# Four chunk operands written in front of the taking of the bonus sum

## The reference

```python
zd = z + mu[d] * (shift_seq(z, offset) - z)            # mixed r, k, v
kk = kk * lax.rsqrt(maximum(sum(kk * kk), 1e-24))      # normed keys
k = k * (1.0 + (a - 1.0) * k_a)
seqs = [r, decay, k, v, -kk, kk * a]                   # go into the scan
bonus = sum(r * k * r_k, axis=-1) * v                  # goes past the scan
```

## Time and profile before

| | us |
|---|---|
| runs, median of 3 (lowest, highest) | 3369.15 (3364.13, 3369.31) |
| profiled execution: span from the first to the last instruction | 3357.8 |
| median of the runs less this span | 11.35 |
| TensorE (PE) busy in the span | 3114.1 (93%) |
| weight loads (PEld) busy | 2493.0 (74%) |
| VectorE (DVE) busy | 1500.2 (45%) |
| ScalarE (ACT) busy | 1162.7 (35%) |
| GpSimd (POOL) busy | 831.6 (25%) |
| mean granted clock of TensorE, share of full speed | 0.976 |

### The profile page before, as it was taken

The page is one execution under the profiler, slowest core; times in us unless marked ns, Lnnn a source line. Parts: engine busy times, 40 slices in busy tenths (PEclk is TensorE's granted clock), DMA queues, the critical chain, the costliest instruction groups (busy, mean ns, idle before and its releaser), DMA issues.

```text
span 3357.8 us, 79208 instructions
## 1 busy us (share of the span) xinstructions
PE 3114.1 (93%) x34382; PEld 2493.0 (74%) x34382; DVE 1500.2 (45%) x2358; ACT 1162.7 (35%) x2403; POOL 831.6 (25%) x518
## 2 busy tenths in 40 slices
PE   7999898999999998999999888989899989989998
PEld 5777676778777786888888666767667667768886
DVE  4455473745444653100144464756565456330033
ACT  4433333423334424211112353434333345342222
POOL 2211111111123132222223221111111243434453
PEclk9999999999999999999999989999999999999999
DMA  5424242434454441111111233413233343522222
GB/s 212 135 97 145 81 142 101 130 121 144 145 166 151 158 169 57 51 63 62 62 50 63 75 101 98 127 63 120 65 122 106 93 140 115 188 69 95 99 88 75
DMA packets 246714, 364.56 MB, mean 109 GB/s; under 512 B 154080, under 2 KB 155376, under 8 KB 245904
## 3 DMA queue, kind: packets, MB, share of 16 engines
q1 hardware_dynamic: 226976, 294.57, 27.6%
q10 hardware_dynamic: 14976, 35.66, 2.7%
q0 software_dynamic: 4464, 29.92, 2.5%
HBM read 290.88 MB, written 69.21 MB: 107 GB/s over the span
## 4 chain that ended last, share of the span: by engine, by line
PE 76%; DVE 6%; issue 5%; ACT 4%; DMA 2%; DVEq 2%; POOLq 2%; PEld 1%; SPq 1%; POOL 0%; PEldq 0%; ACTq 0%
PE banks L281 20%; PE banks L282 18%; PE banks L283 18%; PE banks L1684 2%; PE banks L1023 2%; PE banks L1695 1%; PE banks L1648 1%; PE banks L395 1%; PE banks L1687 1%; PE banks L1745 1%; POOLq L2430 1%; DVE arena L597 1%; PE banks L2057 1%; PE banks L1051 1%; DMA arena<-chunk_inputs 1%
## 5 line engine op out<-in xcount | busy, mean ns | idle before, releaser
L283 PE MATMUL banks<-hx_rounded,slot_rounded 128*128 128x512 f32 (+1 forms) x1624 | 575.1, 354 | 0.0
L906 POOL TENSOR_TENSOR slot_rounded<-slot,branch_weights_high 128x512 fp32r<-128x512 f32 x188 | 251.4, 1357 | 1286.2 <-ACT branch_weights_high L901 1284.9
L281 PE MATMUL banks<-hx_high,weight_parts 128*128 128x512 f32 (+1 forms) x1512 | 537.9, 356 | 10.9 <-DVE hx_low L545 10.4
L281 PE MATMUL banks<-hx_rounded,branch_weights_high 128*128 128x512 f32 (+1 forms) x1280 | 498.8, 390 | 48.1 <-DVE arena L1364 8.6
L282 PE MATMUL banks<-hx_low,weight_parts 128*128 128x512 f32 (+1 forms) x1512 | 538.0, 356 | 0.0
L283 PE MATMUL banks<-hx_high,weight_parts 128*128 128x512 f32 (+1 forms) x1512 | 535.9, 354 | 0.0
L282 PE MATMUL banks<-resid_rounded,branch_weights_high 128*128 128x512 f32 (+1 forms) x1280 | 452.7, 354 | 0.0
L283 PEld LDWEIGHTS banks<-hx_rounded,slot_rounded 128*128 128x128 f32 x1624 | 312.2, 192 | 44.3
L281 PEld LDWEIGHTS banks<-hx_rounded,branch_weights_high 128*128 128x128 f32 x1280 | 245.9, 192 | 128.2 <-issue 75.6
L281 PEld LDWEIGHTS banks<-hx_high,weight_parts 128*128 128x128 f32 x1512 | 286.6, 190 | 55.1 <-issue 14.3
L283 PEld LDWEIGHTS banks<-hx_high,weight_parts 128*128 128x128 f32 x1512 | 286.3, 189 | 41.1
(11 more groups left out here) (263 smaller groups left out, 5853.7 us busy)
## 6 DMA issues: line engine op xcount, KB each, us to landing
slot<-in_w_mix SPq DMA_DIRECT2D x120, 512.0 KB, 3.9
slot<-in_w_ffn_in SPq DMA_DIRECT2D x88, 512.0 KB, 3.3
arena<-chunk_inputs SPq DMA_DIRECT2D x48, 640.0 KB, 4.5
arena<-in_w_ada SPq DMA_DIRECT2D x50, 512.0 KB, 5.1
slot<-in_w_ffn_out SPq DMA_DIRECT2D x44, 512.0 KB, 3.3
slot<-in_w_ada SPq DMA_DIRECT2D x40, 512.0 KB, 4.3
chunk_inputs<-arena SPq DMA_DIRECT2D x80, 256.0 KB, 3.9
arena<-side_projections POOLq DMA_DIRECT2D x16, 1152.0 KB, 6.1
```

Source lines behind the costliest of these rows:

```text
L281: first = nc.tensor.matmul(out, w_hi, x_hi, start=start, stop=False)
L283: return first, nc.tensor.matmul(out, w_lo, x_hi, start=False, stop=stop)
L906: last = nc.gpsimd.tensor_tensor(slots_r[g % 3][:, half], slots[g % 3][:, half], weights_high(g)[:, half], ALU.subtract)
```

## The change

In both directions of every preparation, the four no longer wait for the gap of the bonus. A generator, bonus_taken(until), is called in front of each of them and at the end. It emits the taking (line 1418's instructions, unchanged) at the first call whose bound is not below the bonus's gap; the last call, with 999, emits it in any case. So the taking stands in front of the first of the four whose own gap is not below the bonus's, or behind all four. g now goes on from line 1409's gap. A drain is put in front of the last sum (line 1434). The drain between lines 1427 and 1431, the semaphores and their counts, and the order on the other engines' programs stay.

```diff
                 for d in range(2):
                     k = 8 * d
+                    bonus_left = list(enumerate([s for s in sum_order(l, st, d == 0) if s in outs]))
+
+                    def bonus_taken(until):
+                        while bonus_left and at(("bonus", d)) <= until:
+                            i, s = bonus_left.pop(0)
+                            yield max(g, at(("bonus", d)))
+                            (c0, c1), (t0, t1) = SEGS[s], TSEG[s]
+                            dst = bonus(hq)[:, c0:c1] if d == 0 else TMP[6][:, c0:c1]
+                            dve.wait_ge(pre_prod.sem, pre_prod.ready(l, hq, k + 7 + i))
+                            nc.vector.tensor_tensor(dst, pair(6)[s], TMP[2][:, t0:t1], ALU.mult).then_inc(pre_dve.sem, both_done)
+
...
                     nc.vector.tensor_tensor(TMP[1], TMP[1], E2, ALU.mult).then_inc(made.sem, 1)
 
-                    assert g < at(("bonus", d)), (st, hp, d, g, at(("bonus", d)))
-                    g = at(("bonus", d))
-                    yield g
-                    for i, s in enumerate([s for s in sum_order(l, st, d == 0) if s in outs]):
-                        (c0, c1), (t0, t1) = SEGS[s], TSEG[s]
-                        dst = bonus(hq)[:, c0:c1] if d == 0 else TMP[6][:, c0:c1]
-                        dve.wait_ge(pre_prod.sem, pre_prod.ready(l, hq, k + 7 + i))
-                        nc.vector.tensor_tensor(dst, pair(6)[s], TMP[2][:, t0:t1], ALU.mult).then_inc(pre_dve.sem, both_done)
+                    yield from bonus_taken(g + pace)
                     g += pace
                     yield g
                     nc.vector.tensor_tensor(TMP[0][:, tlo:], TMP[0][:, tlo:], TMP[4][:, tlo:], ALU.mult).then_inc(made.sem, 1)
+                    yield from bonus_taken(g + pace)
                     g += pace
                     yield g
                     nc.vector.scalar_tensor_tensor(out=E3, in0=TMP[7], scalar=-1.0, in1=E3, op0=ALU.mult, op1=ALU.mult).then_inc(made.sem, 1)
+                    yield from bonus_taken(g + pace)
                     g += pace
                     yield g
                     nc.vector.tensor_tensor(TMP[5], TMP[7], TMP[5], ALU.mult)
                     dve.drain()
+                    yield from bonus_taken(g + pace)
                     g += pace
                     yield g
                     nc.vector.tensor_tensor(TMP[5], TMP[5], E2, ALU.mult).then_inc(made.sem, 1)
+                    yield from bonus_taken(999)
+                    g = max(g, at(("bonus", d)))
                 g += pace
                 yield g
+                dve.drain()
                 nc.vector.tensor_tensor(bonus(hq)[:, lo:T], bonus(hq)[:, lo:T], TMP[6][:, lo:T], ALU.add)
```

## The result

The change takes 3383.73 us (median of 5 runs, 3374.91 to 3389.03) against 3369.15: a ratio of 1.0048 with a 95% interval of 1.003 to 1.0066, so it is slower by 0.3 to 0.7%. The forecast was 3387, slower.

The account below looks back on a forecast made before the run. The prediction took TensorE's stream plus its stops as the bound (busy 93% of the span). PRO 10.9, BODY 2.2 and clock 5.1 sum to 18.2 us, on 3369.15 giving 3387 us, range 3373 to 3396.

Parts of the forecast that it names:

- PRO: Opening stage of each layer: the later taking delays TensorE's tile product in four places, 10.9 us (bounds 5.5 and 12.2).
- the first place: PRO, layer 0, direction 0: taking late by the four, two lengthened by GpSimd; 3.9 us (bounds 2.1 and 4.0).
- that second place: PRO, layer 0, direction 1: 0.4 us late, up to 2.2 with GpSimd's pair; 1.6 us taken.
- The block by GpSimd: In PRO, two-SBUF-input VectorE instructions wait for GpSimd reading SBUF; PRO's sum is 10.9 us with it, 5.5 without.
- The bank as the path: Bonus sum and tile products share two banks, so TensorE's next tile product waits for the taking, 6.9 us before the change.
- BODY: Three middle stages of a layer: longer stops less earlier chunk inputs, 2.2 us net (bounds -1 and 4.5).
- the 1.31: TensorE's wait for chunk inputs at 2029.54 in PRO, 1.31 us, claimed to stay because SP issues eight stores before it.
- Clock: Half-clock slices on TensorE after lengthened stops: three times 1.7 us, 5.1 us in all (bounds 0 and 8.5).
- Rival (a): PRO: no block by GpSimd, hardly a clock slice; 9.4 us slower, 3378.5 us; chance 0.20.
- Rival (b): TensorE's stops given back at later stops, no clock cost: 6.5 us, 3375 us, no difference; chance 0.11.
- Rival (c): Faster: TensorE's chunk-input waits decide and go, the late taking costs nothing; 4.5 us less, 3364.7 us; chance 0.04.
- Rival (d): Dearer: the shifted VectorE order also holds up the chain in all BODY stages, above 3396 us; chance 0.03.

Follow-up runs that it names:

- e7: The change, with GpSimd's pair for weight tiles 5 and 8 of each layer waiting until the bonus sum is taken; ratio 1.0038 to the kernel before.
- e3: The change, with the bonus sum of PRO written to banks 4 and 5 instead of those of the tile products; ratio 1.0002 to the kernel before.
- e4: The kernel before, with the bonus sum of PRO in banks 4 and 5; ratio 0.9989 to the kernel before.
- e1: The change in BODY alone, in PRO the taking again in front of the four; ratio 1.001 to the kernel before.
- e6: The change, with all small PRO products in spare banks and the taking before whatever is due at its own gap; ratio 0.9931 to the kernel before.
- e5: The kernel before, with every small product of PRO in banks 0 to 5 instead of the tile products' banks; 3332.45 us, ratio 0.9922.
- e9: The kernel before, with GpSimd's pair for weight tiles 5 and 8 waiting until the bonus sum is taken; ratio 1.0002 to the kernel before.
- e10: The change unaltered, measured again on another chip beside the kernel before; 3381.38 against 3360.8 us, ratio 1.0059.
- e8: The change, but in PRO only two of the four stand in front of the taking, the others behind; ratio 1.0034 to the kernel before.

## Why the prediction was right

**Sign, size and mechanism held.** 18.2 us were forecast, 14.6 measured, 20.6 in the repetition. The terms differ more than the sum.

**PRO, by its four terms.** The additional stops are 4.25, 2.37, 5.56 and 0.43 us, forecast were 3.9, 1.6, 5.2 and 0.2: 12.6 against 10.9. All four came out above the forecast, and two for a slip in it: the row of 2.03 us is 1.08 above 0.95, and I wrote 0.9 for each instruction that GpSimd lengthens. With 1.08 the first place is 2.1 + 2.2 = 4.3 (measured 4.25), and the bound of the second 0.4 + 2.2 = 2.6 instead of 2.2. The one mis-sized by more is that second place, direction 1 of layer 0. I let GpSimd's pair catch one instruction and the end of itself; it caught both, at nearly full price:

```profile
149.80 2.04 DVE L1433 TENSOR_TENSOR arena<-arena 128x769 f32<-128x769 f32 x1
151.91 1.86 DVE L1438 TENSOR_TENSOR arena<-arena 128x769 f32<-128x769 f32 x1
153.69 1.01 DVE L1318 TENSOR_TENSOR arena<-banks,arena 128x512 f32<-128x512 f32 x2
```

The pair does not keep its end while VectorE stands in it. Here it runs from 149.27 for 3.69 us, instead of 2.51, and so still stands beside the second instruction. The bound of 2.2 us for that place was passed by 0.2.

**The block by GpSimd** was weighed from one row and is shown by e7: 0.95 us each without a pair beside them. It is 6.7 of the 12.6 us in PRO; the rest is the time of the four themselves. By the Trainium skill, page SBUF — State Buffer, section Who interferes with whom, a VectorE instruction with two SBUF inputs contends with a GpSimd one that reads SBUF, and one with at most one SBUF input, outside the two-port modes, does not. The traces agree: those of the four that began inside a pair took up to 2.05 us, and the taking, which reads a bank and one SBUF tensor, kept its 0.69 us at 1983.19 inside the pair from 1982.73.

**The bank as the path** was read from the code and the earlier trace rows; e3 with e4 shows it, for the taking was late and the loss of PRO was gone.

**BODY.** The two stops grew by 1.49 and 1.48 us (forecast 1.5 each). The chunk inputs gave back 4.4 us, not 2.2: the 2.24 went whole, though only 1.3 of it was forecast, 0.8 of the 1.31 that I had left standing went too, and the one of 0.43 us I had not counted. By its stops BODY should have cost nothing, yet e1, e3 against e4 and e6 against e5 are 3.6, 5.3 and 2.7 us dearer by the medians (the last not clear of noise). What was forecast for BODY, 2.2 us and one of the three clock stretches of 1.7, is near that, but partly by luck: the gain by the chunk inputs was taken too small, and the clock was counted behind one of the two longer stops. The first of the two stops, in the kernel before and in the change:

```profile
2264.80:2271.60 6.80, 6.72 (x114) 5.18 (x114) 4.09 (x7) 0.51 (x2) 0.00 (x0) 1.00 0.48 145
```

```profile
2282.60:2289.40 6.80, 5.93 (x72) 4.71 (x73) 2.93 (x6) 0.56 (x2) 0.00 (x0) 0.50 0.63 162
```

Behind the stop of 2.05 us TensorE ran at full clock, behind that of 3.54 us at half clock (1.2 GHz) for 6.8 us, in which it lost half of its busy time, about 3 us. The same stands behind the second stop (2449.80, 5.76 us busy). The kernel before had two stretches of 3.4 us there (from 2284.60, behind the wait of 0.93 us that is gone, and from 2431.30), so that about 5.8 less 3.4, 2.4 us, is new in this profile. That is an estimate from one profile of each; it is the size of what the stops leave open.

**Clock.** TensorE is busy 5.3 us longer, 5.1 were forecast. The agreement is luck. Executions that have no longer stop differ by more: e9, with the stops of the kernel before, is busy for 3120.4 us, 6.3 above the profile of the kernel before and 1.0 above that of the change. What stands on more than one profile is the mean granted clock of all runs: 0.9725 in the 6 runs of e10 and 0.9746 in the 17 of the kernel before beside them, which would be 7 us of a TensorE that is always busy, give or take 5 (an estimate from the spread of these runs). The windows of the change around the first stop and around the third:

```profile
111.70:115.10 3.40, 0.96 (x4) 0.38 (x2) 3.40 (x3) 0.09 (x1) 2.19 (x2) 1.00 0.77 240
115.10:121.90 6.80, 4.54 (x11) 3.60 (x12) 4.88 (x7) 0.00 (x0) 0.00 (x0) 0.50 0.37 101
1992.20:1995.80 3.60, 0.00 (x0) 0.00 (x0) 3.60 (x3) 0.83 (x1) 2.99 (x2) 1.00 0.80 222
1995.80:2002.60 6.80, 3.94 (x9) 3.15 (x10) 5.14 (x7) 0.00 (x0) 0.00 (x0) 0.50 0.27 74
```

Both long stops run into 6.8 us at half clock, of which TensorE could lose only the part in which it worked, 4.54 and 3.94 us: 2.3 and 2.0 us. But in layer 1 the kernel before had a stretch at half clock at this place too, behind its stop of 0.95 us:

```profile
1984.20:1987.60 3.40, 3.40 (x9) 2.62 (x9) 3.33 (x4) 0.00 (x0) 1.54 (x1) 0.50 0.84 210
```

That is 1.7 us lost, so the third stop adds only 0.3. And in e10 the same first stop of 4.70 us was followed by 3.4 us at half clock, not 6.8. The step was right in kind, and its size is not shown.

**The rivals.** Rival (a), no block, falls with the 2.04 us instructions. Rival (b), the stops given back later: the waits for ScalarE's line 1216 did not shrink to speak of (30.0 us in all after, 30.6 before); TensorE's idle time rose by 9.9 us where the stops for the taking rose by 15.8 and those for the chunk inputs fell by 4.4. Rival (c), the chunk inputs decide: they gave 4.4 us as priced, but its condition, a taking that holds up no bank, was not there. e3 made that condition in PRO, with the longer stops of BODY still there, and was no faster; nor was e6 against e5, where those stops were 2.67 us instead of 3.54. So (c) seems priced too well even for its own case. Rival (d), above 3396: no run of the change took more than 3389.03.

## What to carry to other kernels

Before work is moved ahead of an instruction that releases a shared buffer, find out who waits for the release, and how long the engine idles in front of it: the move is free only for as much work as fits into that idle time, with the lengthening by a neighbour (here GpSimd) counted in. Here it was worth more to take the shared buffer out of the way: small products in banks of their own, while these lay unused, gave 0.8%, and none of the orders tried on VectorE gained anything, with these banks or without.

## What was not expected of the hardware

Where VectorE and GpSimd meet, both grow: GpSimd's pair took 3.74 us beside two of the four, 2.51 with none of them beside it, and VectorE's instructions 2.04 instead of 0.95. A stop's length alone doesn't tell whether the clock falls. Behind the stop of 2.80 us in e8 half clock follows (first line), behind that of 2.81 us in the change, to 154.52, full clock (second):

```profile
117.70:121.10 3.40, 3.40 (x9) 2.62 (x9) 3.25 (x4) 0.00 (x0) 0.00 (x0) 0.50 0.48 128
```

```profile
154.60:161.40 6.80, 6.80 (x36) 5.84 (x37) 1.06 (x2) 1.08 (x2) 0.00 (x0) 1.00 0.80 207
```

Executions of one kernel differ by more than the change is worth (3354.8 to 3370.6 us in 24 runs of the kernel before on one chip), so that differences of 0.1%, as in BODY, need a dozen runs of each side and still stay near the edge of what can be told.
